# Own queries moved among attention pieces, and forgetting heads' scores made in pairs, in a hybrid attention and expert-retrieval block

## The chip, the cores and the metric

One core of a Trainium2 chip runs the whole program. The metric is the device time of one execution in microseconds (us); the time given for a kernel is the median of its runs. Engines are named as the profile names them: PE is TensorE (PEld its weight loads), DVE is VectorE, ACT is ScalarE, POOL is GpSimd, SP is SyncE, which issues the plain DMAs.

## The reference

512 tokens of width 1024 go through one layer:

```python
h   = x + W_out [ forgetting attention (8 heads of 64) || differential attention (4 heads, two maps of 64 each) ]( W_in norm(x) )
h   = h + retrieval( norm(h) )
out = norm(h) * final_g
```

A forgetting head adds c[q] - c[k] to its scores, where c is the running sum of log sigmoid of a gate (one gate value per head and token), under a causal mask. A differential head is softmax 1 minus lambda times softmax 2, under a mask by chunks of 64. The retrieval: for each token and each of 8 query heads, two searches of 128 sub-keys give 16 numbers out of 16384 experts; each chosen expert has a row u and a row v of 1024; the token's sum is over gelu(u . x) * gate * v. That is 512 x 8 x 16 pairs of rows, gathered from HBM by number.

## The kernel before, in words

The tokens are four tiles of 128. Tile 0 (group 0) is taken through attention, output projection and its first three query heads alone (the list `BEFORE`). Then its retrieval starts, and seven of its eight heads "host" all that is left: the pieces of group 1 (tiles 1 to 3: projections, attention, output projection, half of their queries). What remains then, tile 0's last head and all heads of tiles 1 to 3, is a queue of 400 gathers of 1 MB.

**The hosted stage.** For each head there are 4 groups of 4 experts, and for each group 9 gaps, 252 in all; here they are numbered 0 to 251 (head x 36 + group x 9 + gap). VectorE's program (L1677 to L1696) makes a product with a u row in gaps 0, 2, 4, 6 of a group (`dot`, L1533), an addition of a v row in 1, 3, 5, 7 (`add_row`, L1565), the next head's top-k search in gaps 8 to 17 of a head, and after each gap its part of the pieces that lie there (`pieces_in`, L596). TensorE and ScalarE run the same list of pieces in the same order (L1003, L1263) without the products; ScalarE also makes the GELU of the group before (L1266), in gap 4 (`COLS`), and a gate exponential behind each head's third group. GpSimd issues the gathers of u and v rows into two rings of four (L681, L688), each when VectorE has used the place. Every engine runs its own program in order.

**The planner.** Each piece has a share (L169), its supposed cost. `later`, the list of hosted pieces, is laid out over the gaps by the running sum of the shares (L268 to L276). `keys` of a tile-0 head must lie ahead of that head's search (L274). A piece names its kind, its group and its part: `("query", 0, 2*hd)` is the matmul of one own query head, `("query", 0, 2*hd+1)` the turn (transposes) of it, `("keys", 0, hd)` its sub-key scores, `("project", 1, slab, part)` a projection of tiles 1 to 3.

**Matmul results** go to three PSUM banks in turn, in the order of the list `MM`; a bank is used again when ScalarE or VectorE has emptied it. Attention scores have three banks of their own (`sc_b`); map number k waits until map k - 3 is drained by VectorE (L921). An attention step s makes the scores of item s, the transposed map of item s - 3 and the values of item s - 4 (L900).

**Weight slabs** of 1 MB are loaded by SP in the order of first use (`slab_order`), each when the slab before it in its place has been used for the last time (L615 to L623). Slabs 0 to 17 have six places; the next ones, up to slab 5 of group 1, go round w_ring 0, w_ring 1 and two halves of map_mem (L549 to L557); all later ones alternate by their number in the order between the two places of w_ring.

**Where things lie.** `qT` holds the turned queries of attention and, for tile 0, also the transposed normalized activations from which its retrieval queries are made (L777, L797, L1117). A row-wise own query goes to `staged` (two places, L1143) before its turn. `gfb`, the final gain spread over the partitions, is loaded by SP at L649, between slabs; it is used from L1617 on.

**Forget** of group 1 is one piece behind the projection of slab 3: TensorE's matmul (L836), VectorE's bias and absolute value (L1353, L1356), ScalarE's exp and ln (L1164, L1167), for which VectorE waits (L1356), then VectorE's minimum, running sum and negations (L1358 to L1364). ScalarE's `selq` (L1176) needs them before scores.

## Time and profile before

| | us |
|---|---|
| median of 3 runs | 1546.19 (1545.97 to 1546.67) |
| profiled execution | 1543.74 |
| its span, first to last instruction | 1542.0 |
| PE busy / DVE / ACT / POOL in the span | 1278.2 / 1078.2 / 459.6 / 757.8 |
| DMA | 596.5 MB, mean 387 GB/s |

The stages: tile 0 up to about 101, the hosted stage from there to about 505, then the queue of row gathers. An engine's busy time counts its instructions; a bracket behind a row of a timeline gives the idle time just before it and what ended that. "busy (x)" in a table by stretches is busy time and the number of instructions; PEclk is the granted clock of TensorE as a share of full speed.

### The profile page before, as it was taken

Reading aid. Unit: us, or ns where it says so; the run is one execution under the profiler, and the core shown is the slowest. Engines: PE = TensorE matmul, PEld = TensorE weight load, DVE = VectorE, ACT = ScalarE, POOL = GpSimd, SP = SyncE. Lnnn points to the kernel's source line nnn. Section 1 sums busy time; section 2 is a strip of 40 time slices with the busy share of each in tenths; the row PEclk is TensorE's granted clock in tenths of the full one; section 3 lists DMA queues with packets and bytes.
Section 4 is the critical chain, followed back from the end, with each engine's and each line's share of the span. In section 5 each row is a group of like instructions: output and inputs, shape, how many; then the busy total and the mean of one; then the engine's idle time right before and its main releaser. Section 6 shows DMA issues by size and latency. Waiting matters only on the chain.

```text
span 1542.0 us, 13063 instructions
## 1 busy us (share of the span) xinstructions
PE 1278.2 (83%) x3727; PEld 661.2 (43%) x3727; DVE 1078.2 (70%) x2520; ACT 459.6 (30%) x1200; POOL 757.8 (49%) x637
## 2 busy tenths in 40 slices
PE   9999999988888298999776788777787788777777
PEld 8776655665545144444332333332333333333333
DVE  3257699999988776666666676666666776666654
ACT  3432355466233032222222222221222222222212
POOL 0027477775677444454544544444455454444550
PEclk9999999998989599999999998899999999998999
DMA  9669799997999999999999999999999999999995
GB/s 381 260 248 414 277 324 347 374 376 262 350 362 392 400 391 407 423 421 421 422 421 422 421 422 421 421 422 421 421 421 422 422 421 422 422 421 421 421 421 215
DMA packets 99741, 596.50 MB, mean 387 GB/s; under 512 B 11480, under 2 KB 11480, under 8 KB 42328
## 3 DMA queue, kind: packets, MB, share of 16 engines
q0 software_dynamic: 89856, 536.91, 86.1%
q1 hardware_dynamic: 9816, 58.77, 9.5%
q8 instruction: 31, 0.51, 0.1%
q14 instruction: 38, 0.31, 0.1%
HBM read 593.54 MB, written 2.10 MB: 386 GB/s over the span
## 4 chain that ended last, share of the span: by engine, by line
DMA 43%; PE 15%; DVE 6%; POOL 2%; ACT 2%; issue 2%; DVEq 0%; POOLq 0%
PE acc L993 13%; DMA map_mem<-in_peer_uv_dram,eidx 9%; DMA w_ring<-in_peer_uv_dram,eidx 7%; DMA v_all<-in_peer_uv_dram,eidx 7%; DMA act_mem<-in_peer_uv_dram,eidx 6%; DMA mix_mem<-in_peer_uv_dram,eidx 5%; DMA v_ring<-in_peer_uv_dram,eidx 4%; DMA u_ring<-in_peer_uv_dram,eidx 4%; DMA v_ring<-in_peer_v_dram,eidx 2%; PE mm L785 1%; ACT diag L1226 1%; DVE map_mem L1544 1%; DVE w_ring L1544 1%; PE sc L785 1%; POOL v_ring L691 1%
## 5 line engine op out<-in xcount | busy, mean ns | idle before, releaser
L1219 ACT ACTIVATE gel<-hid 128x4 f32<-128x4 f32 x126 | 25.8, 205 | 713.7 <-DVE hid L1544 704.6
L684 POOL DMA_INDIRECT u_ring<-in_peer_u_dram,eidx x112 | 139.7, 1247 | 171.5 <-DVE eidx L1524 98.6
L993 PE MATMUL acc<-v_all,diag 128*128 128x512 f32 x256 | 128.3, 647 | 65.5 <-ACT diag L1226 65.0
L691 POOL DMA_INDIRECT v_ring<-in_peer_v_dram,eidx x112 | 132.3, 1182 | 64.0 <-DVE h L1572 35.4
L1572 DVE SCALAR_TENSOR_TENSOR h<-v_ring,coef,h 128x1024 f32<-128x1024 f32 x112 | 143.9, 1285 | 16.2 <-DMA v_ring<-in_peer_v_dram,eidx 13.0
L1536 DVE CUSTOM_DVE_ANT_0 u_ring<-u_ring,hn 128x1024 f32<-128x1024 f32 x112 | 136.4, 1218 | 14.0 <-DMA u_ring<-in_peer_u_dram,eidx 13.8
L993 PE MATMUL acc<-v_ring,diag 128*128 128x512 f32 x248 | 123.6, 645 | 27.2 <-ACT diag L1226 23.6
L993 PE MATMUL acc<-u_ring,diag 128*128 128x512 f32 x248 | 123.5, 645 | 26.1 <-ACT diag L1226 24.5
L993 PE MATMUL acc<-map_mem,diag 128*128 128x512 f32 x248 | 120.7, 633 | 25.3 <-ACT diag L1226 25.3
L1226 ACT ACTIVATE diag<-ident,coef 128x128 f32<-128x128 f32 x392 | 126.2, 390 | 48.2 <-DVE coef L1562 39.6
L710 POOL DMA_INDIRECT v_all<-in_peer_uv_dram,eidx x64 | 81.0, 1265 | 89.3 <-PE acc L993 81.4
L710 POOL DMA_INDIRECT map_mem<-in_peer_uv_dram,eidx x62 | 74.8, 1207 | 85.2 <-PE acc L993 78.4
L710 POOL DMA_INDIRECT v_ring<-in_peer_uv_dram,eidx x62 | 75.0, 1209 | 79.9 <-PE acc L993 68.2
L993 PEld LDWEIGHTS acc<-v_all,diag 128*128 128x128 f32 x256 | 51.8, 208 | 137.0 <-issue 137.0
L993 PE MATMUL acc<-w_ring,diag 128*128 128x512 f32 x176 | 88.3, 649 | 25.8 <-ACT diag L1226 25.8
L993 PE MATMUL acc<-act_mem,diag 128*128 128x512 f32 x176 | 88.3, 649 | 25.2 <-ACT diag L1226 25.2
L710 POOL DMA_INDIRECT u_ring<-in_peer_uv_dram,eidx x62 | 74.1, 1195 | 69.9 <-PE acc L993 63.4
L1544 DVE CUSTOM_DVE_ANT_0 map_mem<-map_mem,hn 128x1024 f32<-128x1024 f32 x62 | 75.2, 1223 | 46.3 <-DMA map_mem<-in_peer_uv_dram,eidx 46.3
L1544 DVE CUSTOM_DVE_ANT_0 v_all<-v_all,hn 128x1024 f32<-128x1024 f32 x62 | 75.3, 1223 | 45.9 <-DMA v_all<-in_peer_uv_dram,eidx 45.8
L785 PE MATMUL mm<-act_mem,w_ring 128*128 128x384 f32 x304 | 104.1, 498 | 2.9 <-ACT act_mem L1117 2.9
L1544 DVE CUSTOM_DVE_ANT_0 u_ring<-u_ring,hn 128x1024 f32<-128x1024 f32 x60 | 72.8, 1225 | 42.4 <-DMA u_ring<-in_peer_uv_dram,eidx 42.4
L1544 DVE CUSTOM_DVE_ANT_0 v_ring<-v_ring,hn 128x1024 f32<-128x1024 f32 x60 | 72.8, 1224 | 39.8 <-DMA v_ring<-in_peer_uv_dram,eidx 39.8
(281 smaller groups left out, 2335.9 us busy)
## 6 DMA issues: line engine op xcount, KB each, us to landing
w_ring<-in_slabs_dram SPq DMA_DIRECT2D x29, 1024.0 KB, 8.3
v_ring<-in_slabs_dram SPq DMA_DIRECT2D x6, 1024.0 KB, 11.0
u_ring<-in_slabs_dram SPq DMA_DIRECT2D x6, 1024.0 KB, 11.4
map_mem<-in_slabs_dram SPq DMA_DIRECT2D x6, 1024.0 KB, 8.5
h<-in_x_dram SPq DMA_DIRECT2D x4, 512.0 KB, 13.1
u_ring<-in_peer_u_dram,eidx POOLq DMA_INDIRECT x112, 6.6
v_ring<-in_peer_v_dram,eidx POOLq DMA_INDIRECT x112, 6.9
v_all<-in_x_cols_dram SPq DMA_DIRECT2D x3, 512.0 KB, 7.3
```

Of the source, the lines that this page charges most:

```text
L684: nc.gpsimd.indirect_dma_start(out=u_ring[:, c % U_RING, :], out_offset=None, in_=peer_u[0], in_offset=bass.IndirectOffsetOnAxis(ap=eidx[n ...
L691: nc.gpsimd.indirect_dma_start(out=v_ring[:, c % V_RING, :], out_offset=None, in_=peer_v[0], in_offset=bass.IndirectOffsetOnAxis(ap=eidx[n ...
L710: nc.gpsimd.indirect_dma_start(out=row_mem[place], out_offset=None, in_=peer_uv, in_offset=bass.IndirectOffsetOnAxis(ap=eidx[n % 3][:, c:c ...
L785: last = nc.tensor.matmul(bk[:, 0:n], w[:, c, q * P:(q + 1) * P], actT[:, c, 0:n], start=(c == 0), stop=(c == KC - 1))
L993: last = nc.tensor.matmul(acc[half][:, :], diag[:, c % COLS, :], v_row(n, c)[:, half * BANK:(half + 1) * BANK], start=first, stop=(n % PH ...
L1219: nc.scalar.activation(gel[:, par, g0:g0 + COLS], hid[:, par, g0:g0 + COLS], ACT.Gelu).then_inc(gelu_done, 1)
L1226: nc.scalar.activation(diag[:, c, :], ident[:, :], ACT.Copy, scale=coef[:, par, g0 + c:g0 + c + 1]).then_inc(diag_done, 1)
L1536: nc.vector.tensor_tensor_reduce(out=u_ring[:, c % U_RING, :], in0=u_ring[:, c % U_RING, :], in1=hn[:, :], scale=1.0, scalar=0.0, op0=ALU. ...
L1544: nc.vector.tensor_tensor_reduce(out=u_row(n, c), in0=u_row(n, c), in1=hn[:, :], scale=1.0, scalar=0.0, op0=ALU.mult, op1=ALU.add, accum_o ...
L1572: nc.vector.scalar_tensor_tensor(out=ht, in0=v_ring[:, c % V_RING, :], scalar=coef[:, par, c:c + 1], in1=ht, op0=ALU.mult, op1=ALU.add).th ...
```

## The change

- Own queries of heads 3 to 7 (a matmul, a turn, the keys) are no longer the first hosted pieces. The pieces of group 1 come first, and from a due point for each head its three pieces are put one by one between them.
- `forget` of group 1 becomes three pieces: the matmul, ahead of slab 3; `gate` (bias, absolute value; exp and ln on ScalarE) and `decay` (the rest), behind slab 3.
- Tile 0's transposed activations go to `h0T`, the memory of `gfb`, and its row-wise queries to a buffer of their own, `own_q`. `gfb` is loaded behind the hosted slabs, when the last own query is done.
- Scores of forgetting heads are made at even steps for two heads: first both matmuls with the keys (rows 0 to 63 and 64 to 127 of the array), then both matmuls that add the bias. This holds for tile 0 too.
- ScalarE's GELU of the group before moves from gap 4 to gap 0.

By the planner's arithmetic the pieces come to lie in these gaps:

| piece | before | after |
|---|---|---|
| own query, turn, keys of head 3 | (early), 0, 2 | (early), 20, 20 |
| of head 4 | 0, 2, 4 | 57, 60, 62 |
| of head 5 | 2, 4, 6 | 92, 96, 99 |
| of head 6 | 5, 7, 9 | 126, 129, 131 |
| of head 7 | 7, 9, 10 | 165, 170, 171 |
| first projection of group 1 | 10 | 0 |
| forget matmul / gate / decay | 37 / 37 / 37 | 20 / 27 / 30 |
| first attention step of group 1 | 50 | 40 |
| last forgetting step / first differential step | 140 / 141 | 138 / 139 |
| differential steps 8, 9, 10, 11 | 160, 164, 167, 171 | 158, 161, 166, 171 |
| output projections, slab 12 tile 3 / slab 13 tile 1 | 176 / 178 | 176 / 178 |
| all later pieces | same | same |

and the slabs of w_ring from slab 10 of group 1 on (place 0 or 1; own-query slabs in brackets):

```
before: 10 in 0, 11 in 1, 12 in 0, 13 in 1, 14 in 0
after:  10 in 0, [head 6] in 1, 11 in 0, 12 in 1, [head 7] in 0, 13 in 1, 14 in 0
```

The diff, cut to its core:

```diff
+        gates = [("forget", g)] if g == 0 else [("gate", g), ("decay", g)]
+        ps += fox_in[:values_at] + gates + fox_in[values_at:values_at + 1] + [("selq", g, tiles[0])] + fox_in[values_at + 1:]
+        if g > 0:
+            ps.insert(ps.index(("project", g, 3, 0)), ("forget", g))
...
-    BEFORE, later = first_pieces[:cut_at], first_pieces[cut_at:] + pieces_of(1)
+    BEFORE, own, later = first_pieces[:cut_at], first_pieces[cut_at:], []
+    total, at = sum(share(p) for p in own + pieces_of(1)), 0.0
+    heads = [[p for p in own if p[0] == "query" and p[2] // 2 == hd] + [("keys", 0, hd)] for hd in range(EARLY_HEADS, PH)]
+    due = [(GRP * (i + 1) - 2) / (SLOTS - 1) for i in range(len(heads))]
+    for p in pieces_of(1):
+        if heads and not heads[0]:
+            heads.pop(0)
+            due.pop(0)
+        if heads and at / total >= due[0]:
+            later.append(heads[0].pop(0))
+            at += share(later[-1])
+        later.append(p)
+        at += share(p)
...
+        h0T = gfb[:, :].rearrange("p (c n) -> p c n", c=KC)
+        own_q = sb("own_q", [P, SLAB])
...
-            sp.dma_start(gfb[:, :], ...)
             for n in range(N_IN + N_OUT + 2, len(slab_order) - 2):
                 load_slab(n)
+            sp.wait_ge(mm_full, mm_done(("query", 0, 2 * PH - 2)))
+            sp.dma_start(gfb[:, :], ...)
...
+            def pair_scores(g, step):
+                t, first = at_step(g, 0, step)
+                nk, j = P * (t + 1), GROUPS[g].index(t)
+                if first == 0:
+                    pe.wait_ge(selq_ready, 2 * (t + 1))
+                both = [(HD * (m % 2), m // 2, map_no[(t, m)]) for m in (first, first + 1)]
+                for lo, ch, k in both:
+                    if k >= len(sc_b):
+                        pe.wait_ge(sc_drained, k + 1 - len(sc_b))
+                    nc.tensor.matmul(sc_b[k % len(sc_b)][:, 0:nk], qT[lo:lo + HD, ch, j * P:(j + 1) * P], kv_t[lo:lo + HD, ch, 0:nk],
+                                     start=True, stop=False)
+                for lo, ch, k in both:
+                    nc.tensor.matmul(sc_b[k % len(sc_b)][:, 0:nk], selq[lo:lo + 40, ch, t % 2, :], caug[lo:lo + 40, 0:nk],
+                                     start=False, stop=True).then_inc(sc_full, 1)
...
-                        if gap == COLS and (n or grp):
+                        if gap == 0 and (n or grp):
                             gelu(*group_at(GRP * n + grp - 1))
...
-                    from_act(nc.vector.scalar_tensor_tensor(out=e_f[:, 0:n], in0=z_f[:, 0:n], scalar=-1.0, in1=z_f[:, 0:n],
-                                                            op0=ALU.mult, op1=ALU.max), 2)
+                    nc.vector.scalar_tensor_tensor(out=e_f[:, 0:n], in0=z_f[:, 0:n], scalar=-1.0, in1=z_f[:, 0:n],
+                                                   op0=ALU.mult, op1=ALU.max).then_inc(norm_ask, 1)
+                    rooted[0] += 2
+                    if g == 0:
+                        piece("decay", 0)
+                elif kind == "decay":
+                    g, = p
+                    n, t0 = P * len(GROUPS[g]), P * GROUPS[g][0]
+                    dve.wait_ge(act_norm, rooted[0])
```

## Rows read from the trace of the kernel before

**Rows 1.** Busy time by stretches: microseconds, engines with instruction counts, PEclk, DMA share, GB/s.

```profile
104.00:180.00 76.00, 75.08 (x288) 50.11 (x287) 45.63 (x90) 24.37 (x55) 39.67 (x34) 1.00 0.92 369
180.00:450.00 270.00, 241.49 (x1015) 155.58 (x1014) 258.96 (x541) 136.33 (x326) 193.37 (x158) 0.92 0.93 338
450.00:505.00 55.00, 44.39 (x168) 27.88 (x166) 44.72 (x83) 14.40 (x32) 37.94 (x33) 0.93 0.95 377
700.00:1520.00 820.00, 646.18 (x1341) 268.49 (x1340) 549.45 (x1342) 189.78 (x519) 395.55 (x326) 0.93 1.01 421
```

**Rows 2.** Chain of waits around 525: start, length, what.

```profile
523.68 1.30 DVE h L1572
...
529.94 9.84 PE acc L993 x16
```

**Rows 3.** Waits of DVE, 100 to 510: total us, times, longest.

```profile
DVE u_ring L1536 <- DMA u_ring<-in_peer_u_dram,eidx: 13.8, 12, 3.2
DVE coef L1562 <- ACT gel L1219: 9.7, 3, 4.7
DVE h L1572 <- DMA v_ring<-in_peer_v_dram,eidx: 8.1, 7, 2.2
DVE z_f L1353 <- PE mm L836: 6.9, 1, 6.9
DVE z_f L1358 <- ACT e_f L1167: 2.4, 1, 2.4
...
DVE map_mem L1440 <- PE sc L932: 1.8, 1, 1.8
DVE map_mem L1440 <- PE acc L932: 1.5, 1, 1.5
DVE map_mem L1440 <- PE acc L928: 0.8, 1, 0.8
...
DVE map_mem L1440 <- PE sc L928: 0.4, 1, 0.4
```

**Rows 4.** Timeline of DVE: start, length, line, operation, [idle before <- releaser].

```profile
163.94 0.22 DVE L1562 SCALAR_TENSOR_TENSOR coef<-gel,gate_inv,gexp 128x4 f32<-128x4 f32 x1 [4.52 <-ACT gel L1219]
...
180.73 1.22 DVE L1536 CUSTOM_DVE_ANT_0 u_ring<-u_ring,hn 128x1024 f32<-128x1024 f32 x1
...
454.69 0.22 DVE L1562 SCALAR_TENSOR_TENSOR coef<-gel,gate_inv,gexp 128x4 f32<-128x4 f32 x1 [4.72 <-ACT gel L1219]
```

**Rows 5.** Timeline of PE, 104 to 210.

```profile
106.53 0.41 PE L806 MATMUL mm<-ident,mix_mem 128*128 128x128 f32 x2
...
125.57 5.33 PE L785 MATMUL acc<-act_mem,map_mem 128*128 128x384 f32 x16
...
166.95 5.33 PE L836 MATMUL mm<-act_mem,wf 128*8 128x384 f32 x16
...
193.67 0.48 PE L928 MATMUL sc<-store 64*128 64x256 f32 x1 [0.47 <-ACT v_all L1081]
193.68 0.48 PE L928 MATMUL acc<-store 64*128 64x256 f32 x1
...
208.02 0.70 PE L928 MATMUL acc<-store 64*128 64x256 f32 x2
```

**Rows 6.** Timeline of ACT at the gates of group 1.

```profile
174.15 1.28 ACT L1167 ACT_TABLE_LOAD   x1
```

**Rows 7.** Timeline of PE, output projections.

```profile
381.66 3.60 PE L859 MATMUL mm<-w_ring,store 128*128 128x512 f32 x8
...
411.63 5.37 PE L859 MATMUL mm<-w_ring,store 128*128 128x512 f32 x8 [3.03 <-DVE h L1412]
```

**Rows 8.** Timeline of DVE, the additions of slab 12 tile 3 and slab 13 tile 1.

```profile
391.51 0.68 DVE L1412 TENSOR_TENSOR h<-mm,h 128x512 f32<-128x512 f32 x1
...
394.45 0.68 DVE L1412 TENSOR_TENSOR h<-acc,h 128x512 f32<-128x512 f32 x1
```

**Rows 9.** Instructions on w_ring, 150 to 500: its slab loads, from issue to landing.

```profile
DMA to landing us min/median/max: 5.5/8.1/9.4
```

More of the change, by code:

```diff
@@ L183, in share @@
             return SHARE_ROWS[0] if by_rows else SHARE_COLS[0] + SHARE_COLS[1] * tiles
-        return {"norm1": 4, "xT": 2, "forget": 6, "mix": 4, "mixT": 1, "turn": 1, "selq": 2, "norm2": 4, "hT": 2, "lambda": 1, "lamrow": 1, "squares": 0, "factors": 0, "keys": 1.0 * tiles}[kind]
+        if kind == "forget":
+            return 6 if p[1] == 0 else 0
+        return {"norm1": 4, "xT": 2, "gate": 6, "decay": 0, "mix": 4, "mixT": 1, "turn": 1, "selq": 2, "norm2": 4, "hT": 2, "lambda": 1, "lamrow": 1, "squares": 0, "factors": 0, "keys": 1.0 * tiles}[kind]
     def woven(a, b):
@@ L202, in pieces_of @@
         values_at = fox_in.index(("project", g, 4, 0))
-        ps += fox_in[:values_at] + [("forget", g)] + fox_in[values_at:values_at + 1] + [("selq", g, tiles[0])] + fox_in[values_at + 1:]
+        gates = [("forget", g)] if g == 0 else [("gate", g), ("decay", g)]
+        ps += fox_in[:values_at] + gates + fox_in[values_at:values_at + 1] + [("selq", g, tiles[0])] + fox_in[values_at + 1:]
+        if g > 0:
+            ps.insert(ps.index(("project", g, 3, 0)), ("forget", g))
         if g == 0:
@@ L265, in build @@
     cut_at = first_pieces.index(("keys", 0, EARLY_HEADS - 1)) + 1
-    BEFORE, later = first_pieces[:cut_at], first_pieces[cut_at:] + pieces_of(1)
+    BEFORE, own, later = first_pieces[:cut_at], first_pieces[cut_at:], []
[11 more added lines that the diff above has]
+        at += share(p)
+    assert not any(heads)
     AFTER = [[] for _ in range(SLOTS * GAPS)]
@@ L776, in rows_out @@
                             pe.wait_ge(first_slab, 16)
-                    last = nc.tensor.matmul(bk[:, 0:SLAB], (qT if name[0] == "query" else actT)[:, c, j * P:(j + 1) * P], w[:, c, :],
+                    last = nc.tensor.matmul(bk[:, 0:SLAB], (h0T if name[0] == "query" else actT)[:, c, j * P:(j + 1) * P], w[:, c, :],
                                             start=(c == 0), stop=(c == KC - 1))
@@ L796, in first_query @@
                         for c in range(4 * hf, 4 * hf + 4):
-                            last = nc.tensor.matmul(bks[c2][:, 0:P], w[:, c, c2 * P:(c2 + 1) * P], qT[:, c, 0:P],
+                            last = nc.tensor.matmul(bks[c2][:, 0:P], w[:, c, c2 * P:(c2 + 1) * P], h0T[:, c, 0:P],
                                                     start=(c == 0), stop=(c == KC - 1))
@@ L800, in first_query, with turn @@
                             last.then_inc(mm_full, 1)
-            def turn(name, at):
+            def turn(name, src):
                 bk = mm_bank(name)
                 for q in range(2):
-                    last = nc.tensor.transpose(bk[:, q * P:(q + 1) * P], staged[:, at, q * P:(q + 1) * P], ident[:, :])
+                    last = nc.tensor.transpose(bk[:, q * P:(q + 1) * P], src[:, q * P:(q + 1) * P], ident[:, :])
                 last.then_inc(mm_full, 1)
@@ L822, in piece @@
                     pe.wait_ge(*emptied(("project", g, sl, 0)))
-                    turn((kind, *p), sl % 2)
+                    turn((kind, *p), staged[:, sl % 2, :])
                 elif kind == "forget":
@@ L882, in piece @@
                         pe.wait_ge(*emptied(("query", g, c2 - 1)))
-                        turn((kind, *p), c2 // 2 % 2)
+                        turn((kind, *p), own_q[:, :])
                 elif kind == "keys":
@@ L911, in attend @@
                 values(g, half, step)
+            def pair_scores(g, step):
[12 more added lines that the diff above has]
+                                     start=False, stop=True).then_inc(sc_full, 1)
             def scores(g, half, step):
-                if at_step(g, half, step):
+                if half == 0:
+                    if step % 2 == 0 and at_step(g, half, step):
+                        pair_scores(g, step)
+                elif at_step(g, half, step):
                     t, it = at_step(g, half, step)
                     nk, j = P * (t + 1), GROUPS[g].index(t)
-                    if it == 0:
-                        pe.wait_ge(selq_ready, 2 * (t + 1))
                     for m in maps_of(it):
@@ L1116, in piece @@
                         for c in range(4):
-                            last = nc.scalar.activation((actT if g else qT)[:, 4 * hf + c, j * P:(j + 1) * P], bk[:, c * P:(c + 1) * P],
+                            last = nc.scalar.activation((actT if g else h0T)[:, 4 * hf + c, j * P:(j + 1) * P], bk[:, c * P:(c + 1) * P],
                                                         ACT.Copy, scale=g2c[:, 4 * hf + c:4 * hf + c + 1])
@@ L1159, in piece @@
                     nc.scalar.activation(lam_s[0:1, 2:4], lam_s[0:1, 0:2], ACT.Exp).then_inc(act_norm, 1)
-                elif kind == "forget":
+                elif kind == "gate" or kind == "forget" and p[0] == 0:
                     n = P * len(GROUPS[p[0]])
@@ L1343, in piece @@
                                                 None, ALU.mult).then_inc(factors_ready, 1)
-                elif kind == "forget":
+                elif kind == "gate" or kind == "forget" and p[0] == 0:
                     g, = p
-                    n, t0 = P * len(GROUPS[g]), P * GROUPS[g][0]
+                    n = P * len(GROUPS[g])
                     dve.wait_ge(consts_in, 16 * 7)
```

17 lines of the change are left out of this document (5 added, 12 removed).

## The prediction

> **What bounds the kernel now.** I read the windows by stage first, then the chain of waits, then the timelines of VectorE, TensorE and ScalarE inside the stage that the change touches. [rows 1] show three regimes. From 700 us on the DMA engines stand at a share of 1.01 and 421 GB/s and every compute engine has room: what is left is a queue of 1 MB row gathers, and it ends a fixed time after it has become full. In the hosted stage (104 to 505) the rates are 338 to 377 GB/s, so DMA isn't full there; from 180 to 450 VectorE is, with 259 of 270 us. TensorE shows 241 there as well, but VectorE waits for its scores only 4.5 us in the whole stage [rows 3]. From 104 to 180 VectorE has only 45.6 of 76 us and TensorE 75.1: that part is TensorE's. The chain [rows 2] runs through VectorE's last additions of the hosted stage, at 523.7, and TensorE's first accumulations, at 529.9. So a microsecond that VectorE gains in the hosted stage starts the full DMA queue that much earlier and is a microsecond at the end, less what DMA itself then lacks.
>
> The profiled execution took 1543.74 us (span 1542.0), 2.45 below the median 1546.19. I make the sum on its trace and take the difference from the median.
>
> **The early part.** VectorE stands three times around gap 37: 4.52 us for a GELU [rows 4], 6.9 for the gates' matmul and 2.4 for ScalarE's exp and ln [rows 3], 13.8 us in all. TensorE is why [rows 5]: its first own query work of the stage begins at 106.5, tile 1's projections only at 125.6, the gates at 167.0, the first scores at 193.7. After the change the projections begin at about 106.4 (VectorE has just written their operands by then). A half slab is (166.95 - 125.57) / 8 = 5.17 us, the gates' matmul the 5.33 of its row, a third of a value slab (193.2 - 172.3) / 6 = 3.5. So: six halves to 137.4, a turn, the gates to 143, keys 0.7, two halves to 154, six thirds to 175, scores at about 176.4. That is 18 us earlier for TensorE. But VectorE meets its first scores at gap 40 instead of 50, so the gain isn't 18: it is VectorE's position at gap 40, which is 181.95 before (the end of the product at 180.73) [rows 4] and at best 176.4 after. ScalarE gives the same date. It takes the gates only behind the copy of the last half of slab 3 (154.5) and behind a gate exponential and a GELU; four table loads of 1.28 [rows 6] and five short activations make some 7 us, so ln is done at 161.7. VectorE, at gap 37 by 159.4 before its GELU wait and so at gap 30 by about 150 (seven gaps of some 1.3), waits there some 12 us, then does 2.3 us of decay, and five products and four additions (1.22 and 1.30, [rows 4, 2]), 11.3 us: 175.3. Splitting gate from decay thus moves the wait and doesn't remove it. **Gain 5.4**; bounds: 0 (ScalarE 5 us later) and 13.8 (no wait at all).
>
> **Scores for two heads.** Where two heads' matmuls stand next to each other they already run at the same time: at 193.67 and 193.68 two heads in different rows of the array each take 0.48, while at 208.02 one head alone takes 0.70 for its two [rows 5] and about as much for the two of the bias. A pair at 256 columns then saves some 1.3 us, wider ones more: some 15 us of TensorE for the twelve pairs of tiles 1 to 3. Four and a half own queries, (125.57 - 106.53) / 4.5 = 4.2 us each [rows 5], come into the same stretch, 19 us. These nearly cancel for TensorE, and VectorE is the bound there, so the pairs are worth only VectorE's waits for scores, 1.8 + 1.5 + 0.8 + 0.4 = 4.5 [rows 3]; the second of a pair is ready a step early. A pair also waits for one drain more than a single score did; VectorE is the later one there, so that costs TensorE and not the end. **Gain 4.5**, bounds 0 and 4.5. In tile 0, which is TensorE's, 128 columns should save half of the 1.3; of four pairs one stood together already and one now waits for a drain: **gain 1.2**, bounds 0 and 2.
>
> **GELU at gap 0.** At 454.69 VectorE waits 4.72 us [rows 4] because ScalarE's GELU stands behind the copy of tile 1's first query. At gap 0 it stands ahead of two tiles' transposes and that query. The new wait is ScalarE's, for products that VectorE makes three gaps earlier; queued behind it are copies, which free TensorE's banks, and TensorE has slack. DMA around it is near full (377 GB/s in [rows 1]), so I take **3** of 4.7; bounds 0 and 4.7.
>
> **What the change adds.** First, the slabs. Own-query slabs now go through the two places of the weight ring between projection slabs, so neighbours share a place: slabs 7 and 9 of tiles 1 to 3 have some 10 us of TensorE work to cover a load, slab 11 about 5, and TensorE is ahead of VectorE by more there. One is bare. Output slab 13 falls into the place of slab 12, whose last use is the piece at gap 176; the first use of 13 is the very next matmul group, at gap 178. SP can issue only when the former is done. Before, the two lie in different places and TensorE runs them back to back, the first for 3.60 us from 381.66 [rows 7], while VectorE adds at 391.51 and 394.45 [rows 8]. After: the first ends at about 387 (the query and turn put ahead, 4 us, less two or three gaps by which scores stand earlier); the load lands 8.1 us later (5.5 to 9.4) [rows 9]: 395.4; the matmuls run 3.6, or 5.4 at a dropped clock as at 411.63 after 3 us of idleness [rows 7]: 399 to 401. VectorE wants it at 394.45. Behind it on TensorE stand four attention steps, and VectorE's division for tile 3 at gap 188 needs the last of them; it comes ten gaps later, each with a product or an addition and four with more, so that wait isn't repeated. **Loss 6**, bounds 0 and 12 (a landing of 9.4, half clock, TensorE 4 us late already).
>
> Second, four slabs (4.2 MB, 10 us of DMA at 421) move from before 125 us into 154 to 345, where 338 GB/s [rows 1] leave a fifth of 421 free: a fifth of their 10 us should find no room beside a gather that VectorE waits for. **Loss 2**, bounds 0 and 4 (a fifth more than the 13.8 + 8.1 us that VectorE waits for u and v rows, [rows 3]). Third, the last gain's 0.52 MB is loaded at about 490 instead of 71, into the full queue: 0.524 / 421 = **1.25**, bounds 0 and 1.25. It must be there only for the first output tile, behind the accumulations of [rows 2]. The separate buffer for own queries and the transposed activations in the gain's place cost nothing: the same copies to other addresses.
>
> Sum: 5.4 + 4.5 + 1.2 + 3 - 6 - 2 - 1.25 = 4.85, or 1541.3 us.
>
> The Trainium skill, "DMA: Bandwidth & Descriptors", section "Anatomy of one DMA — SWDGE (gpsimd) path", fits a transfer as about 2.0 us plus its bytes over 436 GB/s; for 1 MB that is an estimate of 4.4 us. The trace doesn't agree for this queue beside gathers: 8.1 us. By the page the slab wait would be 3.7 us shorter and the sum 1537.6.
>
> **The rivals.**
> 1. *The slab is hardly a wait* (0.18). The load lands in 5.5, its fastest, because gathers pause while VectorE stands, and the clock holds: 387 + 5.5 + 3.6 = 396.2 against 394.45, a loss of 1.8 in place of 6, and an early gain somewhat above 5.4: 1535 to 1537. For it: the rows' minimum. Against it: the median. The page's rule above acts in this direction.
> 2. *Nothing is left* (0.24). The stage's end is held by gathers and by GpSimd's issues, which fill 37.9 us and their issue gaps from 450 to 505 [rows 1]; VectorE arrives earlier and waits for rows instead. The 4.5 and the 3 go, the slab's price partly: 1544 to 1548.
> 3. *Slower: the ring's one bare load decides* (0.18). If the slab lands at 9.4, TensorE runs at half clock and is 4 us late, VectorE loses 12, and gap 188's squares, roots and division slip with it. With the early gain at 2 (ScalarE's chain late) that gives 2 + 4.5 + 1.2 + 3 - 12 - 4 - 1.25 = -6.55: 1552.7. It decides from a VectorE wait of some 11 us at gap 178. For it: no matmul stands between the two uses. Against it: VectorE's 6 us of lag behind TensorE there.
> 4. The pairs may not overlap, if the drain between them separates them. It costs the 4.5 and 1.2 and lies inside rival 2.
>
> **How the numbers follow.** The sum as worked out has 0.40 and its own range 1538 to 1543. A measurement of this kernel can tell about 0.2% (3.1 us) from no change, so faster is below 1543.1, slower above 1549.3. The sum and rival 1 are faster (0.58), rival 2 the same (0.24), rival 3 slower (0.18). The range 1533 to 1550 takes in rivals 1 and 2 with the bounds of the small terms, and leaves out most of rival 3 and the far end of the gains.
>
> **What would show it.** Right: projections of tiles 1 to 3 from about 105 us on TensorE, first scores near 175; on VectorE one wait of about 12 us for ln near 150 and none for the gates' matmul; products at gap 40 ending near 176; no wait of VectorE for scores from 200 to 225; no GELU wait near 450; a wait of about 6 us for an output projection near 390, with TensorE idle behind a slab; two heads' scores with starts 0.01 us apart. Wrong: a gap 40 at 180 or later, more than 10 us at gap 178, VectorE waiting for gathers all through 300 to 480, or a full DMA queue that begins where it did before.

## The result, and the profile after

| | us |
|---|---|
| kernel before, median of 20 runs | 1544.74 (1542.56 to 1547.08) |
| kernel after, median of 20 runs | 1547.08 (1543.82 to 1553.07) |
| ratio after to before | 1.0019, 95% interval 1.0012 to 1.0026 |
| span of the profiled execution | 1545.1 (before 1542.0) |

The change makes the kernel 0.19% slower, 2.9 us; 0.32% faster was forecast. Single executions of the kernel after spread over 9 us, those before over 4.5.

VectorE's waits from 100 to 510, which answer to [rows 3]: the four longest, then those for scores and for the gates' matmul (line numbers are those of the kernel after; each experiment has its own):

```profile
DVE u_ring L1573 <- DMA u_ring<-in_peer_u_dram,eidx: 13.6, 14, 3.1
DVE z_f L1395 <- ACT e_f L1197: 13.0, 1, 13.0
DVE h L1449 <- PE acc L880: 6.4, 1, 6.4
DVE h L1609 <- DMA v_ring<-in_peer_v_dram,eidx: 4.5, 7, 1.2
...
DVE map_mem L1477 <- PE sc L962: 2.6, 3, 1.2
DVE map_mem L1477 <- PE sc L947: 2.1, 1, 2.1
...
DVE map_mem L1477 <- PE acc L962: 1.3, 1, 1.3
DVE map_mem L1477 <- PE acc L947: 1.3, 1, 1.3
DVE z_f L1383 <- PE mm L857: 1.0, 1, 1.0
```

The gates' matmul is waited for 1.0 us in place of 6.9, ln 13.0 in place of 2.4, and scores (the four rows of L1477) 7.3 in place of 4.5. New is the wait of 6.4 for an output projection. The GELU waits of [rows 4] are gone. On VectorE's timeline (start, length, line, operation, idle before) the early part stands where it was forecast:

```profile
161.06 0.55 DVE L1395 SCALAR_TENSOR_TENSOR z_f<-z_f,e_f 8x384 f32<-8x384 f32 x1 [13.04 <-ACT e_f L1197]
...
175.87 0.42 DVE L1477 CUSTOM_DVE_ANT_0 map_mem<-sc,act_mem 128x256 f32<-128x256 f32 x1 [1.26 <-PE acc L947]
...
397.41 0.69 DVE L1449 TENSOR_TENSOR h<-acc,h 128x512 f32<-128x512 f32 x1 [6.44 <-PE acc L880]
```

and TensorE's rows show the projections of tiles 1 to 3 from 106, the first scores 19 us earlier than in [rows 5], and the bare load of slab 13 against [rows 7]:

```profile
105.95 10.49 PE L806 MATMUL mm<-act_mem,map_mem 128*128 128x384 f32 x32
...
174.71 0.48 PE L944 MATMUL sc<-store 64*128 64x256 f32 x1 [0.47 <-ACT v_all L1111]
...
379.44 3.60 PE L880 MATMUL mm<-w_ring,store 128*128 128x512 f32 x8
...
392.28 5.10 PE L880 MATMUL acc<-w_ring,store 128*128 128x512 f32 x8 [9.24 <-DMA w_ring<-in_slabs_dram]
```

Counted product by product on the two timelines, VectorE is 4.7 us ahead of the kernel before at 190, still 4.6 ahead at 382, and 3.0 behind at 396, after slab 13. (Times are those of the kernel before.) The GELU wait near 450 is gone and VectorE is level again at 467; but the end of the hosted stage does not follow, as the chain shows, which answers to [rows 2]:

```profile
511.28 15.13 DMA v_ring<-in_peer_v_dram,eidx
526.44 1.29 DVE h L1609
...
532.69 9.98 PE acc L1023 x16
```

The last additions are 2.8 us later (526.44 against 523.68), and so are the first accumulations and the end (3.1). The windows that answer to [rows 1]:

```profile
104.00:180.00 76.00, 75.44 (x284) 49.56 (x283) 50.96 (x102) 25.01 (x54) 42.10 (x36) 1.00 0.85 323
180.00:450.00 270.00, 219.89 (x1010) 147.97 (x1009) 250.28 (x523) 139.99 (x331) 186.40 (x152) 0.92 0.93 346
450.00:505.00 55.00, 48.16 (x175) 29.97 (x173) 47.91 (x89) 15.59 (x33) 39.38 (x34) 0.93 1.00 394
700.00:1520.00 820.00, 644.88 (x1341) 268.64 (x1341) 550.35 (x1347) 190.31 (x521) 396.33 (x326) 0.93 1.01 421
```

From 104 to 180 the DMA engines moved 24.5 MB where they moved 28.0 before (323 and 369 GB/s by 76 us), from 180 to 450 93.4 instead of 91.3. From 450 to 505 they are full (1.00, before 0.95). VectorE has done 5.3 us more of its work by 180 and 3.4 us less of it by 450 (8.7 less in between).

### The profile page after: what moved, and what is told of

The parts are those of the page before. It is cut to its first block, busy times and chain, and to the rows that moved or that the text cites. A ratio compares the mean times of both kernels' runs of the same rounds, so it can differ in the third digit from the quotient of the medians.

```text
span 1545.1 us, 13067 instructions
## 1 busy us (share of the span) xinstructions
PE 1258.2 (81%) x3727; PEld 654.2 (42%) x3727; DVE 1078.5 (70%) x2520; ACT 465.3 (30%) x1205; POOL 757.2 (49%) x637
## 4 chain that ended last, share of the span: by engine, by line
DMA 41%; PE 17%; DVE 5%; POOL 2%; issue 2%; ACT 2%; DVEq 0%; POOLq 0%
PE acc L1023 15%; DMA map_mem<-in_peer_uv_dram,eidx 10%; DMA v_all<-in_peer_uv_dram,eidx 8%; DMA w_ring<-in_peer_uv_dram,eidx 7%; DMA act_mem<-in_peer_uv_dram,eidx 5%; DMA v_ring<-in_peer_uv_dram,eidx 5%; DMA mix_mem<-in_peer_uv_dram,eidx 3%; DMA u_ring<-in_peer_uv_dram,eidx 3%; PE mm L806 2%; DMA v_ring<-in_peer_v_dram,eidx 2%; DVE map_mem L1581 1%; ACT diag L1256 1%; POOL v_ring L712 1%; DVE w_ring L1581 1%; PE sc L806 1%
## 5 line engine op out<-in xcount | busy, mean ns | idle before, releaser
L705 POOL DMA_INDIRECT u_ring<-in_peer_u_dram,eidx x112 | 136.2, 1216 | 179.0 <-DVE eidx L1561 98.3
L712 POOL DMA_INDIRECT v_ring<-in_peer_v_dram,eidx x112 | 135.5, 1210 | 59.8 <-DVE h L1609 30.8
L1023 PE MATMUL acc<-u_ring,diag 128*128 128x512 f32 x248 | 120.2, 630 | 26.0 <-ACT diag L1256 24.5
L1581 DVE CUSTOM_DVE_ANT_0 u_ring<-u_ring,hn 128x1024 f32<-128x1024 f32 x60 | 72.8, 1225 | 41.1 <-DMA u_ring<-in_peer_uv_dram,eidx 41.1
```

The source lines that it names most:

```text
L705: nc.gpsimd.indirect_dma_start(out=u_ring[:, c % U_RING, :], out_offset=None, in_=peer_u[0], in_offset=bass.IndirectOffsetOnAxis(ap=eidx[n ...
L712: nc.gpsimd.indirect_dma_start(out=v_ring[:, c % V_RING, :], out_offset=None, in_=peer_v[0], in_offset=bass.IndirectOffsetOnAxis(ap=eidx[n ...
L1023: last = nc.tensor.matmul(acc[half][:, :], diag[:, c % COLS, :], v_row(n, c)[:, half * BANK:(half + 1) * BANK], start=first, stop=(n % PH ...
L1581: nc.vector.tensor_tensor_reduce(out=u_row(n, c), in0=u_row(n, c), in1=hn[:, :], scale=1.0, scalar=0.0, op0=ALU.mult, op1=ALU.add, accum_o ...
```

## The experiments

All ratios are to the kernel before, with 95% intervals; 0.0010 is 1.5 us. The kernel after is 1.0019. The theories named A to E are set out in the expectations. The interval of a difference between two runs is wider than either's own; where two intervals overlap, the difference is a hint only.

**1. Slab 13 in the other place.**

```diff
-                slab_places.append(n % W_RING)
+                slab_places.append((n + (n > 36)) % W_RING)
```

> The kernel after, with the places of the weight ring exchanged from slab 13 on, so that slab 13 falls into the place of head 7's own-query slab and not into that of slab 12. Both theories: TensorE no longer stands 9.24 us behind a slab near gap 178, and VectorE's wait of 6.44 us at that addition goes. Theory A (bytes: from about 104 us on the end comes when the DMA engines have moved all bytes, so only the time in which they stand idle counts): their idle time from 350 to 440 falls from 12.9 us (8.5 + 4.4) to about the 9.5 of the kernel before, a gain of about 3.4 us on the kernel after: ratio to before 0.9997 (1544.3). Theory B (VectorE: what VectorE gains in the hosted stage comes out at the end, and slab 13's wait took it back): the whole 6.4 us come out: ratio 0.998 (1541.3).

Measured: 1.0010 (1.0001 to 1.0019). The wait of 6.44 us is gone, yet only 1.4 us come out (the intervals overlap), and three other waits of VectorE stand there:

```profile
384.43 0.69 DVE L1477 CUSTOM_DVE_ANT_0 map_mem<-acc,act_mem 128x512 f32<-128x512 f32 x1 [2.49 <-PE sc L962]
428.14 0.69 DVE L1449 TENSOR_TENSOR h<-mm,h 128x512 f32<-128x512 f32 x1 [1.32 <-PE mm L880]
431.58 0.69 DVE L1449 TENSOR_TENSOR h<-mm,h 128x512 f32<-128x512 f32 x1 [1.60 <-PE mm L880]
```

Theory B is out (it wanted 6.4 us), and A's 3.4 is missed too: the DMA engines' share from 350 to 440 is 0.86 as in the kernel after.

**2. An eighth of the own-query slabs' bytes.**

```diff
-                sp.dma_start(slab_mem[place], slabs[sl])
+                part = KC * SLAB // 8 if g == 0 and sl >= N_IN + N_OUT + 4 else KC * SLAB
+                sp.dma_start(slab_mem[place][:, 0:part], slabs[sl][:, 0:part])
```

> The kernel after, in which the own-query slabs of heads 4 to 7 load only an eighth of their 1 MB (the weights of these own queries are then mostly what lay in the place before; all instructions are the same). 3.67 MB fewer are moved, 8.7 us at 421 GB/s. Theory A (bytes): the end comes some 5 to 9 us earlier than in the kernel after, ratio to before 0.996 to 0.999, since those slabs are loaded where the DMA engines are nearly full. Theory B (VectorE): the cost was estimated at 2 us and bounded by 4, so 0 to 4 us: ratio 0.9993 to 1.0019.

Measured: 1.0033 (1.0022 to 1.0044). 3.67 MB less gain nothing, though the DMA engines move 325 GB/s from 154 to 345 where they moved 349: theory A is out as well, and the bytes of these slabs don't bound. (The kernel leaves out seven eighths of these weights, so tile 0's heads 4 to 7 gather other rows, as many of them; what that changes isn't shown.)

**3. GELU at gap 0, alone.**

```diff
-                        if gap == COLS and (n or grp):
+                        if gap == 0 and (n or grp):
```

> The kernel before with one line of the change: ScalarE's GELU at gap 0. Theory B (VectorE): VectorE's waits for it at 454.69 (4.72 us) and 163.94 go, the first passes into the wait for the gates' matmul, the second comes out by about 3 us: ratio 0.998. Theory A (bytes): around 450 the DMA engines are idle for only 2.0 us in 20 (share 0.90 from 440 to 460), so at most 2 us can come out, and VectorE waits for rows in place of the GELU: ratio 0.9987 to 1.0.

Measured: 1.0006 (0.9997 to 1.0014). The 4.72 us at 454.69 are gone. But before that place VectorE falls from 1.5 us behind the kernel before at 258 to 5.7 behind at 450, and stands 0.9 behind once it is past. It now waits where the kernel before does not, or waits less:

```profile
341.61 0.56 DVE L1440 CUSTOM_DVE_ANT_0 map_mem<-sc,act_mem 128x384 f32<-128x384 f32 x1 [2.51 <-PE sc L928]
...
392.16 0.18 DVE L1400 RECIPROCAL rinv<-stat 128x4 f32<-128x4 f32 x1 [1.28 <-ACT stat L1063]
432.20 0.69 DVE L1412 TENSOR_TENSOR h<-mm,h 128x512 f32<-128x512 f32 x1 [1.60 <-PE mm L859]
```

**4. Pairs, alone.** The edit is that of `pair_scores` in the diff above, called at even steps in place of the scores of one head.

> The kernel before with the scores of forgetting heads for two heads at a time, and nothing else. The prediction's terms: 4.5 us in the hosted stage and 1.2 in tile 0, ratio 0.9963. Theory A (bytes): VectorE's 4.5 us of waits for scores lie in stretches in which the DMA engines are 94 to 98 per cent busy, idle for 6 us in 150, so 0 to 3 us: ratio 0.998 to 1.0. A third view, that the second condition on a drained bank gives back what the overlap saves: VectorE's waits for scores stay at 4.5 us or more and the ratio is 1.0 or above.

Measured: 1.0019 (1.0011 to 1.0028): alone they cost 2.9 us. The pairs do overlap: the scores of two heads of tile 1 with their biases, eight matmuls, take 1.14 us together, where one head's four took 1.13 in the kernel before (208.02 in [rows 5], with 0.59 for the bias from 208.56). The step to the first tile with 384 columns shows where that goes. TensorE's timeline and the window from 216 to 222 in the kernel before:

```profile
214.82 0.56 PE L971 MATMUL o<-v_all,map_mem 128*128 128x64 f32 x4
215.21 5.38 PE L785 MATMUL mm<-act_mem,w_ring 128*128 128x384 f32 x16
220.52 0.91 PE L928 MATMUL sc<-store 64*128 64x384 f32 x2
```

```profile
216.00:222.00 6.00, 6.00 (x19) 3.05 (x17) 4.27 (x7) 0.95 (x4) 4.67 (x5) 1.00 0.93 299
```

and with pairs, TensorE and then VectorE:

```profile
208.33 0.48 PE L923 MATMUL acc<-store 64*128 64x256 f32 x1
208.34 0.48 PE L923 MATMUL sc<-store 64*128 64x256 f32 x1
...
209.10 0.37 PE L926 MATMUL sc<-caug,mix_mem 40*128 40x256 f32 x1
...
212.68 0.41 PE L958 MATMUL tr<-ident,map_mem 128*128 128x128 f32 x2 [0.41 <-ACT map_mem L1196]
...
214.87 0.53 PE L958 MATMUL tr<-ident,map_mem 128*128 128x128 f32 x2 [1.38 <-ACT map_mem L1196]
...
215.93 6.63 PE L785 MATMUL mm<-act_mem,w_ring 128*128 128x384 f32 x16
222.49 0.92 PE L923 MATMUL sc<-store 64*128 64x384 f32 x4
...
224.08 0.56 DVE L1449 CUSTOM_DVE_ANT_0 map_mem<-sc,act_mem 128x384 f32<-128x384 f32 x1 [3.41 <-PE sc L926]
```

What TensorE saves it spends idle, 0.41 and 1.38 us, behind ScalarE's maps: 0.3 us behind the kernel before at 208, it is 0.7 behind at 216. Then the next projection takes 6.63 us instead of 5.38, at a granted clock of 0.80 from 216 to 222 (a mean between the levels of 1.2 and 2.4 GHz), where the kernel before has 1.00, and TensorE is 2.0 us behind at 222:

```profile
216.00:222.00 6.00, 6.00 (x16) 3.48 (x16) 4.58 (x7) 0.79 (x5) 4.47 (x6) 0.80 0.91 300
```

and VectorE's first score of that tile is waited for 3.41 us, where [rows 3] had 1.8. The same wait shows 2.10 at 206.32 in the kernel after. (In one profile; for other pairs it wasn't followed.)

**5 to 7. Parts taken out of the kernel after:** slab 13 moved and GELU back at gap 4; the same with single scores; the kernel after with single scores and nothing else changed. The edits are those of 1, of 3 reversed, and of 4 reversed.

> The kernel after with slab 13 in the other place and the GELU back at gap 4 (pairs and the moved own queries kept). Theory C (formed from the first four runs: up to about 440 us VectorE bounds, from there the DMA queue; the 5 us that VectorE gains at gap 40 are given back before 440 by three things: slab 13's place, ScalarE held back by the GELU at gap 0, and the pairs): the GELU of 4.7 us at about 450 comes back as a wait, while VectorE's small waits for scores, statistics and output projections between 330 and 440 shrink by 3 to 4 us; ratio to before 1.0004 or less, against 1.0010 with the GELU at gap 0. The prediction's view (GELU at gap 0 is worth 3 us): slower than with it by 3 us, ratio 1.003.

> The kernel after with slab 13 in the other place, the GELU back at gap 4 and the scores of one head at a time as before: what is left of the change are the moved own queries with their slabs, the divided forget piece and the late load of the last gain. Theory C: the lead of about 5 us at gap 40 now holds until 440, less the own slabs and the 1.25 us of the gain's load: ratio 0.9975 to 0.999. Rival (the own queries among the attention pieces cost in the middle what they gain at its start, whatever the rest does): ratio 1.0 or above, and VectorE's lead on the kernel before falls from 5 us at 200 to 1 or less by 380.

> The kernel after with the scores of one head at a time, everything else as in it. The pairs alone cost the kernel before 0.19%. Theory C: they cost as much here, TensorE stands behind ScalarE's maps for less time, the clock drops less often: ratio 1.000 (against 1.0019). The prediction's view (pairs worth 4.5 and 1.2 us): ratio 1.0055. A third: here the pairs pay for the own queries that lie in the same stretch, so that without them VectorE waits for scores more: ratio above 1.003.

Measured: 1.0047 (1.0034 to 1.0060), 1.0074 (1.0061 to 1.0087), 1.0029 (1.0019 to 1.0039). Theory C is out too: with the own queries moved, the GELU at gap 0 is worth 0.0037 (1.0047 against 1.0010) and the pairs 0.0027 (run 6 against 5) and 0.0010 (run 7 against the kernel after, where the intervals overlap), though neither gains anything in the kernel before. The rival of run 6 came in: VectorE's lead of 4.4 us at 204 is 0.3 at 296 and a lag of 5.3 at 370. From 100 to 510 VectorE waits 15.7 us for scores there, where [rows 3] have 4.5:

```profile
DVE map_mem L1468 <- PE acc L953: 5.8, 2, 4.2
...
DVE map_mem L1468 <- PE sc L949: 4.9, 3, 2.4
DVE map_mem L1468 <- PE sc L953: 3.9, 1, 3.9
...
DVE map_mem L1468 <- PE acc L949: 1.1, 1, 1.1
```

**8. The last gain's load late, alone.**

```diff
-            sp.dma_start(gfb[:, :], ...)
             for n in range(N_IN + N_OUT + 2, len(slab_order) - 2):
                 load_slab(n)
+            sp.dma_start(gfb[:, :], ...)
```

> The kernel before, in which only the load of the last gain (0.52 MB) is moved from 71 us to behind the hosted slabs, near 490. The prediction's view: 0.524 MB at 421 GB/s is 1.25 us in a full queue, ratio 1.0008. Rival: it fits into a gap of the queue, ratio 1.000; or it lies ahead of gathers that VectorE waits for and costs more than its bytes, ratio 1.0015.

Measured: 1.0011 (1.0002 to 1.0019), 1.7 us. The load was issued at 493.4 and landed 11.6 us later.

**9. No own-query slabs for heads 4 to 7** (`lent` names the projection slab used in their place).

```diff
+        if kind == "query" and p[1] == 0 and p[2] >= 2 * (EARLY_HEADS + 1) and slab_used:
+            lent[slab_used] = [x for x in slab_order if x[1] < N_IN][-1]
+            slab_used = lent[slab_used]
...
-                n = slab_order.index((g, sl))
+                n = slab_order.index(lent.get((g, sl), (g, sl)))
```

> The kernel after without the own-query slabs of heads 4 to 7: these four own queries take the projection slab that was loaded last as their weights (so their values are not those of the reference); all matmuls, copies and turns stay where they are, 4 MB are not loaded, and the two places of the ring hold projection slabs alone, as before. Theory D (the two-place ring: own-query slabs between the projection slabs tie TensorE to the landing of slabs, it idles, its clock falls, and VectorE's lead of 5 us at 200 is used up by its waits for scores and output projections): VectorE's waits from 270 to 445 fall from 13 us to 5 or less and the ratio is 0.9985 or less. Rival E (TensorE's and ScalarE's work for the own queries in the attention stretch takes the lead, wherever their weights come from): only slab 13's wait goes, ratio 1.0005 to 1.002, as with slab 13 in the other place (1.0010).

Measured: 1.0005 (0.9996 to 1.0014), which leaves out theory D's 0.9985; VectorE's waits from 270 to 445 are 14.8 us (in a long execution, span 1551.4). Theory D is out but for slab 13: with no own slab of heads 4 to 7 in the ring, VectorE's lead still goes. Counted product by product against the kernel before, it loses 6.8 us between 322 and 386 in this profile; the other ten kernels with moved own queries, the partly moved ones of runs 11 and 13 among them, lose 3.1 to 8.5 there, the eight changed ones with their own queries first 1.0 to 2.6. Part of that may be the one own query itself that lies there.

**10 and 11. Own queries elsewhere.** Both also choose for each slab the place of w_ring whose last use lies further back. Run 10:

```diff
-    due = [(GRP * (i + 1) - 2) / (SLOTS - 1) for i in range(len(heads))]
+    due = [(GRP * (i + 1) + (2.5 if i else -2)) / (SLOTS - 1) for i in range(len(heads))]
```

and in run 11

```diff
+    due = [(GRP * (i + 1) + 2.5 if i > 2 else 0) / (SLOTS - 1) for i in range(len(heads))]
```

> The kernel after with the own queries of heads 4 to 7 some 40 gaps later (gaps 95, 131, 166 and 203 in place of 57, 92, 126 and 165) and each slab in that place of the ring that was used up longer ago; heads 6 and 7 thus lie among output projections and behind them. Theory D: least distance of two slabs in one place 7 gaps once and 9 or more otherwise, where it was 2, 7, 11, 11: ratio 0.999. Rival E: two of four own queries leave the attention stretch, but lie among output projections, which VectorE also waits for: ratio 1.000 to 1.002.

> The kernel after with the own queries of heads 3 to 5 among the first pieces (gaps 0 to 25), those of heads 6 and 7 at gaps 166 and 203, and each slab in the place used up longer ago: none among the attention steps of the forgetting heads. Rival E: VectorE's lead at 200 is smaller (2 us), but it keeps it, ratio 0.998 to 0.9995. Theory D: the same, since the ring's distances are 9 gaps or more but for one of 7. If the ratio is above 1.001, the cost lies neither in the ring nor in the attention stretch.

Measured: 1.0012 (1.0003 to 1.0021) and 1.0003 (0.9994 to 1.0012). Slab 13's bare load is gone in both, so they compare with run 1 (1.0010): later alone gains nothing on it, and three heads early may gain 0.0007, with overlapping intervals.

**12 and 13. The gain's load earlier,** in the version of run 1 (n is 37) and in that of run 11 (n is 41).

```diff
             for n in range(N_IN + N_OUT + 2, len(slab_order) - 2):
+                if n == 37:
+                    sp.wait_ge(mm_full, mm_done(("query", 0, 2 * PH - 2)))
+                    sp.dma_start(gfb[:, :], ...)
                 load_slab(n)
```

> The kernel after with slab 13 in the other place (1.0010) and the load of the last gain put ahead of slab 13's, near gap 165, where the DMA engines are idle for a sixth of the time, and not into the full queue near 490. Its price in the kernel before was 0.11% (1.0011). If that is the price of bytes in the full queue: ratio 1.0000. If it is the price of something else, or the load holds up slab 13: 1.001 or above.

> The version with the own queries of heads 3 to 5 early and of heads 6 and 7 at gaps 166 and 203 (1.0003), with the load of the last gain put behind that of head 7, near gap 203, and not into the full queue near 490. If the load costs what it did in the kernel before and in the version with slab 13 in the other place (0.0011 to 0.0019): ratio 0.9985 to 0.9992, below the kernel before. If that was chance: 1.0003.

Measured, run 12: 0.9991 (0.9982 to 1.0001), 0.0019 less than run 1, with the load issued at 374.0 and landed in 7.0 us. Run 13: 1.0005 (0.9995 to 1.0014), no less than run 11, with the load at 437.0.

**14. Own queries first, all else as after.**

```diff
-    BEFORE, own, later = first_pieces[:cut_at], first_pieces[cut_at:], []
...
+    BEFORE, later = first_pieces[:cut_at], first_pieces[cut_at:] + pieces_of(1)
```

> The kernel after with the own queries of heads 3 to 7 first among the hosted pieces, as before; the pairs, the divided forget piece, the GELU at gap 0 and the late load of the last gain stay. It takes the moved own queries, and with them slab 13's place, alone out of the change. If the move is what costs (with single scores and the GELU at gap 4 the moved queries stood at 1.0074): ratio 0.998 to 1.000. If the parts that were tried alone add up (pairs 0.0019, GELU 0.0006, gain load 0.0011): ratio 1.0036. The prediction's view (the move gains 5.4 us early and loses 8 later, so that without it the time is 2.6 us less): ratio 1.0002.

Measured: 0.9996 (0.9987 to 1.0005). The move alone, with the slab order that it brings, costs 0.0023, or 3.6 us: more than the whole loss.

**15. Forget divided, alone** (the lines of `gates`, "forget", "gate" and "decay" in the diff above, with the shares of these pieces); **16. with the GELU at gap 0.**

> The kernel before with forget of tiles 1 to 3 in three pieces (matmul ahead of slab 3, gate, decay) and nothing else. The prediction's view: the wait for the gates' matmul (6.9 us) and for ln (2.4) turn into a wait for the first scores, which TensorE makes at 193 whatever the gates do: ratio 1.000. Rival: the scores of tile 1 start by the length of the gates' chain earlier, 2 to 5 us: ratio 0.997 to 0.999. Another: the gates' exponential on ScalarE lies ahead of copies that TensorE needs, ratio above 1.001.

> The kernel before with forget in three pieces and the GELU at gap 0: own queries first, single scores, the gain's load at its old place. If the two add (0.9991 and 1.0006): 0.9997. If GELU at gap 0 is worth something once VectorE has come out of its wait for the gates' matmul (the divided kernel still waits 10.3 us for a GELU between 165 and 270): 0.997 to 0.9985, below both kernels.

Measured: 0.9991 (0.9982 to 1.0000) and 1.0007 (0.9998 to 1.0016).

**17. Slab 13 in slab 12's place, alone** (the diff of run 1 in the kernel before).

> The kernel before with only the places of the ring exchanged from slab 13 on, so that slab 13 falls into slab 12's place: the bare load by itself. The prediction's view: VectorE waits about 6 us for the addition near gap 178 and all of it comes out at the end: ratio 1.004. From the step between the kernel after and the one with slab 13 in the other place (1.0019 to 1.0010): the wait is there, but the row gathers fill the rings of four in it, and what comes out is 1 to 3 us: ratio 1.0007 to 1.002. If the ratio is 1.000, the wait is wholly hidden.

Measured: 1.0029 (1.0017 to 1.0041), 4.5 us. TensorE and then VectorE, against [rows 7, 8]:

```profile
392.48 6.44 PE L859 MATMUL acc<-w_ring,store 128*128 128x512 f32 x8 [7.51 <-DMA w_ring<-in_slabs_dram]
...
398.96 0.69 DVE L1412 TENSOR_TENSOR h<-acc,h 128x512 f32<-128x512 f32 x1 [4.71 <-PE acc L859]
```

The wait of 4.71 us comes out about whole. Slab 13's load took 7.4 us from issue to landing here and 9.2 in the kernel after. The Trainium skill, "DMA: Bandwidth & Descriptors", section "Anatomy of one DMA — SWDGE (gpsimd) path", has a fit for DMAs of the GpSimd path, by which 1 MB is an estimate of 4.4 us. SP issues these loads, so the fit is not one for them, and the two times don't agree with it.

**18. Own queries first, gain's load early** (run 14 with the lines of run 12; n is 28).

> The version with the own queries first and all else as after (0.9996), in which the last gain is loaded near 170 us, as soon as the transposed activations that share its memory are used, and not near 490. If the late load costs 0.0011 as it did in the kernel before: ratio 0.9985. If it costs nothing when the rest of the change is there (as in the version with three early and two late own queries): 0.9996. Against the divided kernel with the GELU at gap 0, this one differs by the pairs alone: pairs that cost 0.0019 here as well would put it that much above.

Measured: 0.9978 (0.9969 to 0.9987), median 1540.54: below both kernels, 0.0018 less than run 14. The load was issued at 126.5 us, earlier than stated in the expectation. Its longest waits of VectorE from 100 to 510 besides rows:

```profile
DVE z_f L1383 <- ACT e_f L1185: 9.8, 1, 9.8
...
DVE rinv L1425 <- ACT stat L1081: 1.8, 3, 1.3
DVE rinv L1473 <- PE o L989: 1.7, 1, 1.7
DVE h L1437 <- PE mm L868: 1.6, 1, 1.6
```

Its one profile does not carry the gain: the first accumulation starts at 529.77 (before 529.94).

## Why the prediction was wrong

A gain of 4.85 us was forecast, from a median of 1546.19 in three runs (twenty give 1544.74), and 2.9 were lost, so 7.8 us have to be accounted for. VectorE's waits, summed by stretch from the view of waits of each profile (us):

| kernel | ratio | 104-165 | 165-270 | 270-445 | 104-445 |
|---|---|---|---|---|---|
| before | 1 | 20.5 | 12.6 | 4.7 | 37.8 |
| forget divided (15) | 0.9991 | 15.5 | 15.2 | 7.3 | 38.0 |
| own first, gain early (18) | 0.9978 | 17.2 | 11.5 | 9.2 | 37.9 |
| own first, rest as after (14) | 0.9996 | 19.4 | 13.3 | 7.6 | 40.3 |
| after | 1.0019 | 23.0 | 5.1 | 13.0 | 41.1 |
| slab 13 moved (1) | 1.0010 | 23.2 | 6.8 | 10.5 | 40.5 |
| and gain early (12) | 0.9991 | 23.1 | 5.5 | 13.5 | 42.1 |
| own queries later (10) | 1.0012 | 23.0 | 5.4 | 13.5 | 41.9 |
| slab 13 moved, GELU back (5) | 1.0047 | 20.4 | 10.3 | 14.7 | 45.4 |
| and single scores (6) | 1.0074 | 20.2 | 13.0 | 13.8 | 47.0 |

Kernels whose own queries come first wait 4.7 to 9.2 us from 270 to 445, those with all of them moved 10.5 to 14.8. What the move saves from 165 to 270 it loses there and at ln before 165. The last column ranks the kernels only roughly. One profile stands behind each row, and executions differ: the kernels after, (1) and (12) are the same program up to 370 us, yet their waits from 165 to 345 are 7.9, 10.4 and 13.4, and the first product of the stage ends 3.8 us later in (1) than in the kernel after.

- **The early part: right as a date.** First scores were drained at 175.87 (forecast 176.4), VectorE waited 13.04 us for ln (some 12), and stood 4.7 us earlier at 190 (5.4). Divided forget alone is worth 1.4 us, with an interval down to 0, where it was counted as nothing by itself.
- **Slab 13: right as a wait, not as a price in this company.** The term was 6; the wait was 6.44 in the kernel after (its load took 9.2 us, 8.1 forecast) and 4.71 by itself, where it cost 4.5 us. In the kernel after only 1.4 us came back on moving it, because other waits take its place.
- **The move as a whole: nearly right, by luck.** Its terms, 5.4 - 6 - 2, made a loss of 2.6; measured 3.6 (run 14 against after). But slab 13 stands in that with 1.4 in place of 6, and the slabs' bytes, the reason of the 2, cost nothing that run 2 shows. By these figures some 7 us (an estimate, 4.7 + 3.6 - 1.4) were lost to what no term had. The loss between 322 and 386 without own slabs (run 9) speaks for the own queries' work on TensorE and ScalarE among the attention pieces; it isn't shown apart from the rest, as the intervals of runs 9 and 14 overlap.
- **This step failed: "These nearly cancel for TensorE, and VectorE is the bound there".** On it rests that 19 us of own queries in the attention stretch cost nothing but slabs, and that each other part is worth the wait of VectorE that it removes: "so the pairs are worth only VectorE's waits for scores", 4.5, with 1.2 in tile 0 and 3 for the GELU 8.7 us, less 1.25 for the gain's load.

  With the own queries first, all of that together, with the divided forget, is run 14: 0.6 us gained (by its interval between 2.0 gained and 0.8 lost) where 7.45 were forecast, and that is 6.85 of the 7.8 us. With the own queries moved, the pairs are worth 4.2 (run 6 against 5) and the GELU 5.7 (run 5 against 1); but the moved queries without both and without the bare load (run 6) lost 11.4 us, where the terms left there, 5.4 - 2 - 1.25, made a gain of 2.15. So the parts hang together, and the sum had no term for that; which of them the loss is charged to depends on the order in which they are taken out.

  In its place the runs show that VectorE was not the only bound: TensorE had hardly any room either, 241 of 270 us in [rows 1], and itself stood behind ScalarE's maps for 0.41 and 1.38 us in run 4. Waits for scores were 7.3 us after, not 0, and 15.7 in run 6. In the kernel before, most of the GELU's 4.72 us was lost again by 450 (run 3), and the pairs cost 2.9 us; where they were followed, TensorE's time saved became idleness and a lower clock. Tile 0's 1.2 can't be seen: the first product of the stage ends 0.3 us earlier in the kernel after and 1.7 later in run 4, within what executions differ by.
- **The gain's load: perhaps a little small.** Forecast 1.25 with 1.25 as its bound; 1.7 alone, 2.9 and 2.8 when it was moved forward in runs 12 and 18, nothing in run 13, where it went only to 437. Each of the four, taken with its interval, allows 1.25. In the kernel after it was issued at 497.0 and landed 11.4 us later, beside the last gathers that the chain runs through.
- **The end.** That the queue ends a fixed time after its start holds roughly: from the first accumulation to the end of the span it is 1010.4 to 1012.9 us in all profiles. That a microsecond gained by VectorE in the hosted stage starts it earlier does not: VectorE is 2.5 and 2.1 us ahead of the kernel before at 480 in runs 14 and 18, and 0.3 behind and 0.2 ahead at 540.
- **The rivals.** Rival 1 is out, with 6.44 us of wait and not 1.8. Rival 2 said that VectorE would arrive earlier and wait for rows instead. It did not arrive earlier, but from 467 on it did lose time in that way: level with the kernel before at 480, 2.8 us behind at 526, with the DMA engines full. Rival 3's mechanism was there at 6.4 us of its 12. Rival 4 is out: the pairs overlap.

What stays open: run 18 is 0.0029 faster than run 16. It differs by the pairs, by the buffers `h0T` and `own_q` and by the place of the gain's load; these weren't tried one by one, and pairs alone had cost 0.0019. Nor is it shown why ScalarE's GELU order matters so much more beside moved queries, or which of TensorE and ScalarE holds VectorE there.

## What to carry to other kernels

When two engines are both nearly full in a stage, a wait of one is not a price: ask what the other engine will wait for once it is gone, and add up the waits of the whole stage in the trace instead of the wait that an edit removes. Small edits of this kind aren't additive; take each out of the finished version and not only put each into the old one, as here nearly every part changed its sign or its size with its company. And try transfers that nobody needs soon ahead of a full queue, not in it: moving 0.5 MB gave 2.9 and 2.8 us in two of three tries, and was the cheapest gain here.

## What the runs showed of the hardware

Idleness of TensorE of 0.4 and 1.4 us (run 4) was followed by a granted clock of 0.80 over 6 us and a projection of 6.63 us in place of 5.38, so that the engine, 0.3 us behind the kernel before ahead of the overlapped heads, was 2.0 behind at the next ones. A load of 0.52 MB took 11.4 us from issue to landing in the full queue at 497, 7.0 and 7.3 at 374 and 437, and 9.3 and 12.1 at 71 and 126 us. Its cost at the end, 1.7 to 2.9 us in three comparisons and nothing in a fourth, doesn't follow these times. A load of 1 MB on the SP queue beside row gathers took 7.4 and 9.2 us (slab 13 in run 17 and in the kernel after).
